# Expert gathers of the second table six steps behind the first table's, in place of four

## The chip, the cores and the metric

The kernel runs on one core of a Trainium2 chip. The metric is the device time of one execution in microseconds (us), lower is better. Engines are named as in the profile: PE is TensorE (matmul, with its weight loads as PEld), DVE is VectorE, ACT is ScalarE, POOL is GpSimd, SP is SyncE, which here only issues DMAs.

## What is computed

Two transformer layers over 256 tokens of width 2048. All but the last part is dense: convolution, attention, gating, feed-forward. The change touches only the last part, a layer of 16,384 one-neuron experts, cut here from the reference:

```python
top_s, top_pos = lax.top_k(cand, PEER_TOPK)              # 16 experts per head, 8 heads, each token
expert_idx = jnp.take_along_axis(cand_idx, top_pos, axis=-1)
gates = jax.nn.softmax(top_s, axis=-1).astype(xn.dtype)
...
u = jnp.take(expert_u, idx, axis=0)                      # one row of 2048 floats per expert
a = jnp.einsum('thkd,td->thk', u, xb)
hid = jax.nn.gelu(a) * g
vsel = jnp.take(expert_v, idx, axis=0)
return jnp.einsum('thk,thkd->td', hid, vsel)
```

So each token needs 128 rows of table u, a dot product with each, and then the same 128 rows of table v, weighted and summed.

## The kernel before

**Steps and groups.** 128 tokens lie on the partitions, and there are two such token tiles. One step k gathers one expert's row for each of 128 tokens: `gather_u(k)` brings 128 rows of table u into one of `NU` = 5 slots (`s_u`), `gather_v(k)` 128 rows of table v into one of `NV` = 7 slots (`s_v`). There are 256 steps; four steps are a group g, so group g has steps 4g to 4g+3, and there are 64 groups. Experts with a first key of 88 or more (5120 of them, 40 panels of 128) are not gathered: their rows are skipped by the bounds check, and they are computed densely for all tokens from panels that SP loads.

**What each engine does with a step.** DVE does `dot(k)`: two fused multiply-and-sum instructions over 1024 columns each (L1706), which also frees the u slot. After the four dots of a group, `dots_summed(g)` (L1718) lets ACT apply the gelu (L1097); DVE multiplies by the gates in `hidden(g)` (L1756), which stands behind the first dot of group g+1; ACT then spreads the result into small diagonal matrices, `spreads(g)` (L1050). PE does `adds(k)` (L2291), four matmuls with the v slot as the moving operand, which adds the weighted rows into PSUM and frees the v slot. The trace shows each such matmul as two rows, so one add is x8.

**What surrounds them on PE.** PE runs its program in order: iteration i is for the adds of group i-1. In iterations 0 to 16 the dense u panels stand between the adds (L2240, 40 of them), in iterations 18 to 31 the "token fours" (L2280, 64 of them, which make the gates of the dense experts), from iteration 34 on the dense v panels (L2250, 40 of them). I call these the first, the second and the third stage.

**The handshake of the second stage.** For each token four, DVE and ACT build one-hot operands. On DVE they stand between the dots, in program order. The part that the prediction turns on is `one_keys_late` (L1738), once in a group, behind dot 4g+1: it overwrites the buffer of the group before, and so waits on `one_key_used` until PE has run all token fours of iteration g-1. These stand behind the adds of group g-2, of which the last is add 4g-5. `gated` (L1749) has a similar wait.

```python
for q in range(4):                          # PE, iteration i
    if i >= 1:
        adds(4 * (i - 1) + q)
...
for f in token_fours_in(i)[-4:]:
    token_four(f)
```

**The order of the gathers.** POOL issues all gathers, in an order written out in one loop. `gather_u(k)` waits until dot k-5 has freed its slot (`dot_ready`), `gather_v(k)` until add k-7 has freed its slot (`v_used`). POOL stands still while it waits, and whatever stands behind waits too. `LAG` says how many steps `gather_v` runs behind `gather_u`:

```python
gather_u(0)
gather_v(0)
gather_v(1)
for k in range(1, ROUTES * TOPK + LAG):
    if k < ROUTES * TOPK:
        gather_u(k)
    for first in {4: (2, 3), 5: (4, 5), 6: (6,)}.get(k, ()):
        gather_v(first)
    if k >= LAG + NV:
        gather_v(k - LAG)
```

Of the kernel before, what the change touches and what calls it, by code (L numbers as in the profile page):

```python
# [214 lines left out]
def two_layers(nc, stream, dense_u, columns, x, meta, b_out, g_mix_post, g_ffn, g_ffn_post, g_norm1, g_norm2, w_forget,  # L215
# [9 lines left out]
    def place(name, shape, offset, dt=f32):  # L225
        assert name not in names
        names.add(name)
        return nc.alloc_sbuf_tensor_at(name, shape, dt, offset=offset)
# [95 lines left out]
    panel_early = [place(f"s_panel_early{i}", [128, D], S + k * K) for i, k in enumerate((60, 52, 32))]  # L324
    NE = len(panel_early)
    score = place("s_score", [128, TT * PH, 2 * NKEYS], S + 16 * K)
    NU, NV, NW, NH, BATCH, LAG = 5, 7, 4, 4, 4, 4
    ROUTES, GROUPS = TT * PH, TOPK // BATCH


# [2069 lines left out]
```

How the kernel before makes its waits and increments, by code:

```python
def wait(engine, semaphore, value):  # L209
    if not (isinstance(value, int) and value <= 0):
        engine.wait_ge(semaphore, value)
# [239 lines left out]
        @block.sync  # L452
# [2 lines left out]
            for t in range(TT):  # L455
                sp.dma_start(xres[:, t, :], x[t * 128:(t + 1) * 128, :]).then_inc(x_loaded[t], 16)
            sp.dma_start(cols[:, :], columns).then_inc(cols_loaded, 16)
            for s in range(4):
                sp.dma_start(raw[s][:, :], stream[s]).then_inc(raw_loaded[s], 16)
            panels = stream.rearrange("(q s) p n -> q s p n", s=4)
            with sp.Fori(1, NPANELS // 4) as q:
                for s in range(4):
                    sp.wait_ge(panel_used, q * 4 + (s - 4 + 1 + 1))
                    sp.dma_start(raw[s][:, :], panels[bass.ds(q, 1), s].rearrange("a p n -> (a p) n"))\
                        .then_inc(raw_loaded[s], 16)
            for d in range(NE, 2 * DENSE):
                if d == DENSE:
                    sp.wait_ge(panel_used, NPANELS + 1 + DENSE)
                    sp.dma_start(xn_late[:, :], put_by[0]).then_inc(xn_back, 16)
                    sp.dma_start(xres_late[:, :], put_by[1]).then_inc(xres_back, 16)
                if d < NE + 2:
                    sp.wait_ge(split_ready, NSPLITS - 3 + d - NE)
                else:
                    sp.wait_ge(panel_used, NPANELS + 1 + d + 1 - 2)
                src = dense_u[d] if d < DENSE else expert_v[(SPARSE + d - DENSE) * NKEYS:(SPARSE + d - DENSE + 1) * NKEYS, :]
```

## Time and profile before

| | us |
|---|---|
| median of 3 executions | 3002.77 (2999.91 to 3003.15) |
| the profiled execution, its own time | 3000.82 |
| its span in the trace | 2998.8 |
| PE busy in the span | 2758.8 (92%) |
| DVE busy | 1923.8 (64%) |
| ACT busy | 1178.2 (39%) |
| POOL busy | 652.6 (22%) |

Positions in the trace are microseconds from the start of the span. The first gather is issued at 1804.95 and the last at 2976.76, so the change can act only in the last 1,200 us. A row of a timeline reads: start, duration, engine, line, instruction, output<-input, count, and in square brackets how long the engine stood idle before it and what ended that. In a row of stages each engine has its busy time and number of instructions, then come the granted share of the TensorE clock, the mean busy share of the 16 DMA engines, and what they moved in GB/s.

### The profile page before, as it was taken

To read this page: it belongs to the slowest core of one execution; us is meant where nothing else is said; L and a number is where in the kernel's file an instruction comes from. 1 tells how busy PE (TensorE), PEld (TensorE's weight loads), DVE (VectorE), ACT (ScalarE), POOL (GpSimd) and SP (SyncE) were. 2 spreads that over 40 slices of the span, in tenths; PEclk is the share of its full clock that TensorE was granted. 3 is DMA by queue.
4 is the path that set the end of the run, shared out by engine and by line. 5 is a ranking of instruction groups with operands and counts; after the bars stand their busy time and mean duration, and the time that the engine had idled before them with its cause. 6 is when DMAs were issued, how large, how long until landed. Compare 5 with 4: busy or idle time off the path is not lost.

```text
span 2998.8 us, 45605 instructions
## 1 busy us (share of the span) xinstructions
PE 2758.8 (92%) x17100; PEld 2069.8 (69%) x17100; DVE 1923.8 (64%) x3184; ACT 1178.2 (39%) x2298; POOL 652.6 (22%) x568
## 2 busy tenths in 40 slices
PE   8999999999999997999999999999977887887884
PEld 7886788888888887989999889777754432222230
DVE  6888566556656565455444558987869875555555
ACT  1003443333334344435334444655556542222223
POOL 0000000000000000040000002444447664444453
PEclk9999999999999998999999999999977678998996
DMA  6333545555555553443455657999999999999998
GB/s 244 141 141 106 206 161 187 184 194 182 191 187 187 190 184 129 155 155 141 177 186 184 239 200 259 363 418 409 416 383 396 390 416 417 415 413 394 414 407 319
DMA packets 131299, 785.52 MB, mean 262 GB/s; under 512 B 34631, under 2 KB 34631, under 8 KB 35847
## 3 DMA queue, kind: packets, MB, share of 16 engines
q1 hardware_dynamic: 55424, 393.68, 35.6%
q0 software_dynamic: 75712, 389.74, 32.3%
q8 instruction: 94, 1.54, 0.2%
q14 instruction: 69, 0.56, 0.1%
HBM read 940.23 MB, written 4.19 MB: 315 GB/s over the span
## 4 chain that ended last, share of the span: by engine, by line
PE 57%; DMA 19%; DVE 12%; issue 7%; ACT 3%; POOL 2%; DVEq 1%; POOLq 0%; SPq 0%; ACTq 0%
DMA s_u<-in_expert_u,s_u_index 15%; PE bank L1847 10%; PE bank L1841 10%; PE bank L1842 10%; PE bank L1843 10%; PE bank L1848 5%; PE bank L1937 4%; PE bank L2240 4%; DVE s_u L1706 4%; DMA s_v<-in_expert_v,s_v_index 3%; PE bank L2291 2%; POOL s_u L585 2%; DVE s_cacc L1217 2%; DVE s_w_lo L1128 1%; DVE s_yrow L1390 1%
## 5 line engine op out<-in xcount | busy, mean ns | idle before, releaser
L1128 DVE TENSOR_TENSOR s_w_lo<-s_raw,s_w_hi 128x2048 fp32r<-128x2048 f32 x258 | 592.6, 2297 | 578.0 <-ACT s_w_hi L628 577.6
L628 ACT ACTIVATE s_w_hi<-s_raw 128x2048 fp32r<-128x2048 f32 x256 | 490.4, 1916 | 751.7 <-PE bank L1843 476.3
L1847 PE MATMUL bank<-s_a,s_w_hi 128*128 128x512 f32 x1408 | 493.8, 394 | 3.4 <-DVE s_w_lo L1128 3.2
L1706 DVE CUSTOM_DVE_ANT_0 s_u<-s_u,s_xn_late 128x1024 f32<-128x1024 f32 x256 | 303.7, 1224 | 244.0 <-DMA s_u<-in_expert_u,s_u_index 217.1
L2291 PE MATMUL bank<-s_v,s_spread 128*32 128x512 f32 x2048 | 310.3, 715 | 152.0 <-DMA s_v<-in_expert_v,s_v_index 121.6
L1050 ACT ACTIVATE s_spread<-s_ident,s_hid 32x32 f32<-32x32 f32 x1024 | 325.7, 318 | 205.0 <-DVE s_hid L1756 175.8
L1848 PE MATMUL bank<-s_a,s_w_lo 128*128 128x256 f32 x1408 | 394.8, 280 | 0.0
L585 POOL DMA_INDIRECT s_u<-in_expert_u,s_u_index x256 | 292.5, 1142 | 432.1 <-DVE s_halfdot L1706 267.9
L601 POOL DMA_INDIRECT s_v<-in_expert_v,s_v_index x256 | 309.9, 1211 | 191.7 <-PE bank L2291 109.6
L1706 DVE CUSTOM_DVE_ANT_0 s_u<-s_u,s_xn 128x1024 f32<-128x1024 f32 x256 | 303.8, 1224 | 56.0 <-DMA s_u<-in_expert_u,s_u_index 49.6
L1841 PE MATMUL bank<-s_a,s_w_hi 128*128 128x256 f32 x1152 | 325.3, 282 | 4.1 <-DVE s_a L1152 2.4
L1842 PE MATMUL bank<-s_a,s_w_hi 128*128 128x256 f32 x1152 | 324.6, 282 | 0.0
L1843 PE MATMUL bank<-s_a,s_w_lo 128*128 128x256 f32 x1152 | 324.2, 281 | 0.0
L1847 PEld LDWEIGHTS bank<-s_a,s_w_hi 128*128 128x128 f32 x1408 | 264.3, 188 | 66.5 <-DVE s_w_lo L1128 6.4
L2291 PEld LDWEIGHTS bank<-s_v,s_spread 128*32 128x32 f32 x2048 | 64.1, 119 | 345.0 <-issue 267.0
L2250 PE MATMUL bank<-s_raw,s_ha 128*32 128x512 f32 x2560 | 298.9, 616 | 0.2 <-DMA s_raw<-in_expert_v 0.2
L2240 PE MATMUL bank<-s_xnt,s_raw 128*128 128x256 f32 x1184 | 264.8, 382 | 2.9 <-ACT s_ha L1060 1.7
L1848 PEld LDWEIGHTS bank<-s_a,s_w_lo 128*128 128x128 f32 x1408 | 264.6, 188 | 0.4
L2240 PEld LDWEIGHTS bank<-s_xnt,s_raw 128*128 128x128 f32 x1184 | 222.1, 190 | 59.6 <-issue 28.2
L1937 PE MATMUL bank<-s_a_f,s_raw 128*128 128x272 f32 x1024 | 235.2, 393 | 2.1 <-DVE s_a_f L1185 1.4
L2250 PEld LDWEIGHTS bank<-s_raw,s_ha 128*32 128x32 f32 x2560 | 97.6, 115 | 201.6 <-issue 195.7
L1841 PEld LDWEIGHTS bank<-s_a,s_w_hi 128*128 128x128 f32 x1152 | 218.0, 189 | 8.5 <-issue 4.4
(321 smaller groups left out, 3821.8 us busy)
## 6 DMA issues: line engine op xcount, KB each, us to landing
s_raw<-in_stream SPq DMA_DIRECT2D x292, 1024.0 KB, 4.7
s_raw<-in_expert_v SPq DMA_DIRECT2D x40, 1024.0 KB
s_raw<-in_dense_u SPq DMA_DIRECT2D x37, 1024.0 KB
s_u<-in_expert_u,s_u_index POOLq DMA_INDIRECT x256
s_v<-in_expert_v,s_v_index POOLq DMA_INDIRECT x256
s_panel_early<-in_dense_u POOLq DMA_DIRECT2D x3, 1024.0 KB, 11.4
s_xres<-in_x SPq DMA_DIRECT2D x2, 1024.0 KB, 5.9
out<-s_out_row SPq DMA_DIRECT2D x32, 64.0 KB
```

The source lines that it names most:

```text
L628: act.activation(w_hi[s % 2][:, :], raw[s][:, :], ACT.Copy).then_inc(hi_ready, 1)
L1128: dve.tensor_tensor(w_lo[s % 2][:, :], raw[s][:, :], w_hi[s % 2][:, :].bitcast(f32), ALU.subtract)\
L1706: ins = dve.tensor_tensor_reduce(out=u_slot[k % NU][:, half], in0=u_slot[k % NU][:, half], in1=xn_late[:, half] if t else xn[:, 0, half], ...
L1841: pe.matmul(dst, left[0], right[0], start=start, stop=False)
L1842: pe.matmul(dst, left[0], right[1], start=False, stop=False)
L1843: return pe.matmul(dst, left[1], right[0], start=False, stop=stop)
L1847: pe.matmul(dst, left[0], both, start=start, stop=False)
L1848: return pe.matmul(dst[:, 0:T], left[1], both[:, 0], start=False, stop=stop)
L1937: ins = pe.matmul(bank[c][:, 0:L], raw[c % 4][:, k * 128:(k + 1) * 128], a_f[:, k, :], start=k == 0, stop=k == KT - 1)
L2240: ins = pe.matmul(bank[b][:, 0:T], source[:, k * 128:(k + 1) * 128], xnt[:, k, 0:T], start=k == 0, stop=k == KT - 1)
L2250: ins = pe.matmul(bank[4 * t + q][c * Q:(c + 1) * Q, :], ha[:, d, t * 128 + q * Q:t * 128 + (q + 1) * Q], raw[r][:, c * 512:(c + 1) * 512] ...
L2291: ins = pe.matmul(bank[4 * t + q][c * Q:(c + 1) * Q, :], spread[g % NW][:, q, :], v_slot[k % NV][:, c * 512:(c + 1) * 512], start=False, s ...
```

## The change

`LAG` goes from 4 to 6. Every `gather_v` from the eighth on (v7) is issued two steps of `gather_u` later, and the last six stand behind the last `gather_u`, where it was four. The first seven `gather_v`, the slots, the waits of each gather and all other engines' programs stay as they are.

```diff
     score = place("s_score", [128, TT * PH, 2 * NKEYS], S + 16 * K)
-    NU, NV, NW, NH, BATCH, LAG = 5, 7, 4, 4, 4, 4
+    NU, NV, NW, NH, BATCH, LAG = 5, 7, 4, 4, 4, 6
     ROUTES, GROUPS = TT * PH, TOPK // BATCH
```

What that makes of POOL's queue at the start, from `gather_u(9)` on, where `s_u0` to `s_u4` are the u slots (step k uses slot k modulo 5) and `s_v0` to `s_v6` the v slots (modulo 7). Before:

```order
L585 DMA s_u4_137<-in_expert_u,s_u_index2_177 128x2048
L585 DMA s_u0_133<-in_expert_u,s_u_index2_177 128x2048
L585 DMA s_u1_134<-in_expert_u,s_u_index2_177 128x2048
L601 DMA s_v0_138<-in_expert_v,s_v_index1_192 128x2048
L585 DMA s_u2_135<-in_expert_u,s_u_index0_175 128x2048
L601 DMA s_v1_139<-in_expert_v,s_v_index2_193 128x2048
L585 DMA s_u3_136<-in_expert_u,s_u_index0_175 128x2048
L601 DMA s_v2_140<-in_expert_v,s_v_index2_193 128x2048
```

The same place on POOL in the changed kernel:

```order
L585 DMA s_u4_137<-in_expert_u,s_u_index2_177 128x2048
L585 DMA s_u0_133<-in_expert_u,s_u_index2_177 128x2048
L585 DMA s_u1_134<-in_expert_u,s_u_index2_177 128x2048
L585 DMA s_u2_135<-in_expert_u,s_u_index0_175 128x2048
L585 DMA s_u3_136<-in_expert_u,s_u_index0_175 128x2048
L601 DMA s_v0_138<-in_expert_v,s_v_index1_192 128x2048
L585 DMA s_u4_137<-in_expert_u,s_u_index0_175 128x2048
L601 DMA s_v1_139<-in_expert_v,s_v_index2_193 128x2048
```

The gather v7 (slot `s_v0`) stood behind u11 (slot `s_u1`) and stands behind u13 (slot `s_u3`) now.

In the second stage, POOL's queue around v95 (slot `s_v4`), the last gather that the adds of group 23 need. Before:

```order
L585 DMA s_u4_137<-in_expert_u,s_u_index5_180 128x2048
L601 DMA s_v4_142<-in_expert_v,s_v_index4_195 128x2048
L585 DMA s_u0_133<-in_expert_u,s_u_index6_181 128x2048
L601 DMA s_v5_143<-in_expert_v,s_v_index5_196 128x2048
L585 DMA s_u1_134<-in_expert_u,s_u_index6_181 128x2048
L601 DMA s_v6_144<-in_expert_v,s_v_index5_196 128x2048
```

The same place in the changed kernel, which begins with the same `gather_u(99)`:

```order
L585 DMA s_u4_137<-in_expert_u,s_u_index5_180 128x2048
L601 DMA s_v2_140<-in_expert_v,s_v_index4_195 128x2048
L585 DMA s_u0_133<-in_expert_u,s_u_index6_181 128x2048
L601 DMA s_v3_141<-in_expert_v,s_v_index4_195 128x2048
L585 DMA s_u1_134<-in_expert_u,s_u_index6_181 128x2048
L601 DMA s_v4_142<-in_expert_v,s_v_index4_195 128x2048
```

v95 stood behind u99, which waits for dot 94; it stands behind u101 now, which waits for dot 96.

## Rows read from the trace of the kernel before

**Rows 1.** The page's first part: busy time of each engine.

```profile
PE 2758.8 (92%) x17100; PEld 2069.8 (69%) x17100; DVE 1923.8 (64%) x3184; ACT 1178.2 (39%) x2298; POOL 652.6 (22%) x568
```

**Rows 2.** Busy time by stage: start:end, length, engines, PE clock, DMA share, GB/s.

```profile
1880.00:1890.00 10.00, 8.30 (x46) 5.77 (x45) 9.05 (x25) 4.45 (x12) 3.01 (x4) 1.00 0.81 280
1890.00:1900.00 10.00, 10.00 (x54) 7.17 (x52) 9.21 (x30) 7.86 (x29) 3.84 (x5) 1.00 0.90 338
1900.00:2203.00 303.00, 301.52 (x1607) 218.13 (x1606) 242.80 (x663) 164.09 (x524) 145.46 (x125) 1.00 1.01 414
2240.00:2260.00 20.00, 18.79 (x124) 10.77 (x123) 15.96 (x30) 10.70 (x33) 9.63 (x8) 0.76 0.76 280
2260.00:2340.00 80.00, 62.85 (x370) 35.49 (x373) 77.06 (x147) 51.12 (x155) 62.52 (x46) 0.69 1.01 410
2425.00:2700.00 275.00, 227.87 (x1896) 71.95 (x1899) 154.57 (x288) 84.73 (x272) 145.14 (x128) 0.89 1.01 415
2700.00:2975.00 275.00, 210.32 (x1728) 64.99 (x1720) 152.64 (x282) 81.75 (x263) 135.73 (x122) 0.85 1.00 405
```

**Rows 3.** DMA queues and issues from 1900 to the end.

```profile
q0 software_dynamic: 70506, 358.67, 80.4%
...
s_v<-in_expert_v,s_v_index POOLq DMA_INDIRECT x246
s_u<-in_expert_u,s_u_index POOLq DMA_INDIRECT x242
...
s_xn_late<-put_by SPq DMA_DIRECT2D x1, 1024.0 KB, 8.4
```

**Rows 4.** Timeline of POOL at the start: v7 and v9.

```profile
1885.45 0.99 POOL L601 DMA_INDIRECT s_v<-in_expert_v,s_v_index  x1 [0.30 <-issue]
...
1896.19 0.99 POOL L601 DMA_INDIRECT s_v<-in_expert_v,s_v_index  x1 [0.30 <-issue]
```

**Rows 5.** Waits of POOL and PE, 1900 to 2203: total us, times, longest.

```profile
POOL s_v L601 <- PE bank L2291: 82.8, 25, 10.0
...
PE bank L2240 <- DMA s_raw<-in_dense_u: 1.2, 2, 0.7
```

**Rows 6.** Chain that ended last: two gathers of u, issue to landing.

```profile
2034.43 22.95 DMA s_u<-in_expert_u,s_u_index
...
2184.71 21.10 DMA s_u<-in_expert_u,s_u_index
```

**Rows 7.** Timeline of POOL, second stage: v91, v93, v95, v97.

```profile
2290.07 0.99 POOL L601 DMA_INDIRECT s_v<-in_expert_v,s_v_index  x1 [0.30 <-issue]
...
2295.31 1.97 POOL L601 DMA_INDIRECT s_v<-in_expert_v,s_v_index  x1 [0.31 <-issue]
...
2303.49 0.99 POOL L601 DMA_INDIRECT s_v<-in_expert_v,s_v_index  x1 [0.30 <-issue]
...
2309.33 1.97 POOL L601 DMA_INDIRECT s_v<-in_expert_v,s_v_index  x1 [0.30 <-issue]
```

**Rows 8.** Timeline of PE: adds 91 and 95 and the token fours behind them.

```profile
2302.31 1.07 PE L2291 MATMUL bank<-s_v,s_spread 128*32 128x512 f32 x8 [1.10 <-DMA s_v<-in_expert_v,s_v_index]
...
2305.11 1.96 PE L2280 MATMUL bank<-s_one_key,s_one_key_late 128*128 128x40 f32 x16
...
2316.23 1.94 PE L2291 MATMUL bank<-s_v,s_spread 128*32 128x512 f32 x8 [2.93 <-DMA s_v<-in_expert_v,s_v_index]
...
2321.53 3.61 PE L2280 MATMUL bank<-s_one_key,s_one_key_late 128*128 128x40 f32 x16
```

**Rows 9.** Timeline of DVE: `one_keys_late` of groups 24 and 25.

```profile
2310.37 1.21 DVE L1738 TENSOR_TENSOR s_one_key_late<-s_iota_f,s_slots_t 128x1024 f32<-128x1024 f32 x1
...
2325.41 1.22 DVE L1738 TENSOR_TENSOR s_one_key_late<-s_iota_f,s_slots_t 128x1024 f32<-128x1024 f32 x1
```

**Rows 10.** Chain that ended last: the last gather, v255, and its add.

```profile
2976.76 14.89 DMA s_v<-in_expert_v,s_v_index
...
2991.79 1.10 PE bank L2291 x8
```

## The prediction, on record before the changed kernel ran

> **What bounds the kernel now.** The first view is the page's busy time [rows 1]: PE is busy for 92% of the span and everything else far less, which says nothing about the last 1,200 us, where alone the change can act. So the second view is the busy time by stage [rows 2]. The reader is to see three different limits there. From 1900 to 2203, the stage with the dense u panels, PE is busy for 301.52 of 303 us, and the DMA engines are full at the same time (share 1.01, 414 GB/s). From 2260 to 2340, in the stage with the token fours, DVE is busy for 77.06 of 80 us, and the DMA engines are again full (410 GB/s). From 2425 on, PE and DVE have room, and the DMA engines alone are full (415 and 405 GB/s). Two stretches are not full: 1880 to 1900 (shares 0.81 and 0.90) and 2240 to 2260 (0.76).
>
> The third view is the list of DMA queues and issues [rows 3]: 358.67 MB in 246 + 242 gathers is 0.735 MB a gather, and at 414 GB/s that is 1.78 us of the DMA engines' time. A gather that isn't issued while they have room costs 1.78 us later, when they are full; the two steps of the change are worth 3.6 us. The fourth is the chain that ended last: a gather of u takes 22.95 and 21.10 us from its issue to its landing [rows 6], some twelve times its own transfer. The rest is queue. All gathers together move the same bytes before and after, so the end can only move by time in which the DMA engines have less to do than now, or more.
>
> **The change part by part.** No instruction is added or removed. Only `gather_v` moves, in POOL's queue, behind two more `gather_u`; SP's queue is not touched. I go through the stages.
>
> *Start.* v7 now issues at 1885.45. Its new place is behind u13, where v9 now issues at 1896.19 [rows 4], so v7 comes 10.7 us later, and each v after it similarly. The u gathers around it gain nothing, for there they wait for dots (DVE is busy 9.05 and 9.21 of 10 us). Two gathers less are moved while the DMA engines have room: a loss between 0 (they catch up before it matters) and 3.6 us. The queue fills at once afterwards, so I take more than half, +2 us.
>
> *First stage.* `gather_v` stands still for PE here 25 times, 82.8 us in total, up to 10.0 us [rows 5], and a `gather_u` behind it stands too. With the change two more `gather_u` are out before POOL stops. That looks like the gain, but PE has waited for its panels for only 1.2 us in this stage and the DMA engines are full, so neither has time to give back. What can change is the order: u rows come up to 3.6 us earlier against the same bytes, and the first dot of the second stage (u72, which takes 21.10 us to land) with them. Between 0 and -3.6 us; I take -1, since the start has taken away most of it. The adds keep up: a v gather is issued seven adds ahead, nearly two groups of PE's work, and two gathers less of lead leave them in time.
>
> *Second stage.* Here is the term that decides. Behind the first two dots of group g, `one_keys_late` waits until PE has run the token fours of iteration g-1, and these stand behind add 4g-5. Now gather v(4g-5) stands behind u(4g-1), which waits for dot 4g-6. With the change it stands behind u(4g+1), which waits for dot 4g-4. So a circle of seven dots becomes one of five: dot 4g-4, POOL's issue, the landing, the add, four token fours, `one_keys_late`. Is there room for that? For group 24, v91 issues at 2290.07, and its new place is where v93 stands, 2295.31: 5.2 us later [rows 7]. The add starts when v91 has landed, 2302.31, the fours end at 2305.11 + 1.96 = 2307.07 [rows 8], and DVE comes to `one_keys_late` at 2310.37 [rows 9]: 3.3 us of room, so 1.9 us late. For group 25, v95 goes from 2303.49 to v97's place at 2309.33, 5.8 us later; the add starts at 2316.23, the fours end at 2321.53 + 3.61 = 2325.14, DVE is there at 2325.41: 0.3 us of room, so 5.6 us late. The mean of these two is 3.8 us. What is queued behind `one_keys_late` on DVE is every later dot, so all `gather_u`, and behind those all `gather_v`.
>
> There are 11 such groups (21 to 31). The wait of group g depends on dot 4g-4, which is behind `one_keys_late` of group g-2 and ahead of that of group g-1, so delays add up over every second group: 5.5 x 3.8 = 21 us if the landing takes as long as now. That is the upper end. It will not: when DVE stalls, fewer gathers are under way, and they land sooner. Now v91 lands within 2302.31 - 2290.07 = 12.2 us and v95 within 12.7. The shortest 1 MB landing near this stage is 8.4 us, for `xn_late` [rows 3]. With 8.4, v91 is not late any more (1.9 - 3.8), v95 still 5.6 - 4.3 = 1.3 us: mean 0.6, 5.5 x 0.6 = 3.5 us. The lower end is 0, as nothing excludes that landings shorten by a little more. I take 6, nearer to the 8.4 us case. It can't be made good later, as the DMA engines are full to the end.
>
> Of a landing the Trainium skill gives another picture (DMA: Bandwidth & Descriptors, section on the anatomy of one DMA on the gpsimd path): a fixed 2.0 us and the bytes at 436 GB/s. By that page the estimate for a gather is 3.7 us, the stage would have room for two steps more, and this term would be 0. The rows don't agree with it for a full queue (12.2 to 22.95 us), though they may come nearer to it as the queue empties; this is what the second rival below rests on, by its own rows.
>
> *Third stage.* DMA-bound; PE waits little for spreads, and a v slot's round trip is seven steps in either kernel. 0. The bound for a gain: if the 405 GB/s of 2700 to 2975 rose to the 415 of the stretch before, 275 x (1 - 405/415) = 6.6 us.
>
> *End.* v255 is issued at 2976.76, lands 14.89 us later, and its add starts at 2991.79 [rows 10]. It waits for add 248. v248 comes two u gathers later in the queue, but u252, whose dot opens its group, two v gathers earlier. I take 0; at most +3.6.
>
> The sum is 2 - 1 + 6 + 0 + 0 = +7 us. Against the profiled execution's own time that is 3000.82 + 7 = 3007.8 us. The median of the runs shown is 2 us higher, 3002.77, so I predict 3002.77 + 7 = 3010 us. A difference of under 0.2% (6 us) is about what a measurement of this kernel can't tell from no change, and my forecast is just outside of it.
>
> **The rivals.**
> 1. *No change that can be told.* The landings of the second stage shorten by as much as the gathers come late, and the two gathers of the start are made good by the order. For it: v91 needs only 1.9 us. Against it: v95 needs 5.6, and DVE has only 3 us of room in 80. Time: 3002.8 to 3006, the start's 3.6 at most.
> 2. *Faster.* The two extra u gathers under way do what the first stage's waits suggest, and fill the hole of 2240 to 2260, where 20 x (1 - 0.76) = 4.8 us of DMA time are idle. With the 3.6 us of the first stage that is 3002.8 - 8.4 = 2994 us. For it: 82.8 us of POOL's waits. It decides if the idle DMA time before 2260 is smaller after than before and that of the second stage no larger. Against it: in that hole DVE waits in its handshake with PE, which two more gathers of u don't release.
> 3. *Much slower.* The landings stay at 12 us and the circle costs the full 21 us, with 2 more for the start: 3025 us. Against it: a DMA queue that is not fed can't stay as long as one that is.
>
> That the change does nothing at all is excluded by POOL's order, of which each place after v6 differs.
>
> **How the numbers follow.** I give my forecast (a moderate loss in the second stage) 0.38, rival 1 0.33, rival 2 0.17, rival 3 0.12. Slower by over 0.2%: rival 3 and nine tenths of the forecast, 0.46. Faster: 0.17. Within 0.2%: 0.37. The likeliest case by itself spans 3006 to 3015. The range goes from rival 2's price, 2994, to rival 3's, 3025, with about 1 in 10 beyond each.
>
> **What would show it.** In the changed kernel's profile: DVE's idle time ahead of `one_keys_late`, now next to nothing, is 5 us or more over the stage, released by PE's token fours; PE's idle time ahead of adds 91 and 95 ends with a landing; the landing of v95 takes 8 to 11 us in place of 12.7; the DMA share from 2260 to 2425 falls by 2 to 5%; the first stage's end on PE stays within 2 us; POOL's waits for PE in the first stage fall to under half. The prediction is wrong if DVE is not stalled there and the end moves all the same, or if PE, in the first stage, comes to wait for v gathers, which I have put at nothing.

## The result, and the profile after

The changed kernel takes 3024.61 us (median of 6 runs, 3022.07 to 3026.43) against 3001.84 us before (6 runs on the same chip, 2999.67 to 3003.15). The ratio is 1.0076, with a 95% interval of 1.0066 to 1.0087: slower by 22.8 us, or 20 to 26. I had forecast slower, by 7 us. The direction and the place are right, and the size is a third of what came. The time lies 0.4 us inside the upper end of my range, 3025, and that end was the price of a rival whose mechanism did not come. That the range holds is luck.

The profiled execution took 3025.01 us, with a span of 3023.0 us. The page's busy time, which answers to [rows 1], does not show the loss: every engine does the same work.

```profile
PE 2780.3 (92%) x17100; PEld 2075.3 (69%) x17100; DVE 1922.3 (64%) x3184; ACT 1178.6 (39%) x2298; POOL 654.0 (22%) x568
```

The busy time by stage does. These rows of the changed kernel answer to [rows 2], with the same columns (start:end, length, five engines, PE clock, DMA share, GB/s).

```profile
1880.00:1890.00 10.00, 8.38 (x47) 5.84 (x46) 9.12 (x25) 4.40 (x11) 2.02 (x3) 1.00 0.75 259
1890.00:1900.00 10.00, 10.00 (x55) 7.33 (x54) 9.13 (x30) 7.93 (x29) 2.87 (x4) 1.00 0.82 282
1900.00:2203.00 303.00, 298.57 (x1579) 217.04 (x1581) 242.67 (x663) 163.94 (x524) 141.43 (x125) 1.00 1.01 411
2203.00:2260.00 57.00, 43.43 (x228) 27.50 (x228) 37.46 (x71) 28.15 (x83) 20.31 (x19) 0.61 0.84 326
2260.00:2340.00 80.00, 62.02 (x336) 33.24 (x330) 70.95 (x133) 48.94 (x149) 54.93 (x42) 0.64 0.97 373
2340.00:2425.00 85.00, 63.89 (x332) 33.28 (x328) 70.41 (x136) 47.48 (x142) 55.39 (x44) 0.60 0.94 365
```

And two windows of the kernel before that the prediction had not read:

```profile
2203.00:2260.00 57.00, 37.10 (x233) 24.93 (x229) 43.19 (x80) 32.74 (x98) 25.19 (x22) 0.67 0.90 353
2340.00:2425.00 85.00, 65.76 (x350) 34.29 (x342) 75.03 (x142) 49.35 (x148) 58.05 (x48) 0.62 0.99 394
```

The reader is to see three things. In the start, from 1880 to 1900, the DMA engines move 259 and 282 GB/s in place of 280 and 338, which is 0.77 MB or about one gather less, and in the first stage 411 in place of 414. From 2203 to 2425 they move much less: 326, 373 and 365 GB/s in place of 353, 410 and 394. And DVE, busy for 77.06 of 80 us before, is busy for 70.95: it waits. From 2260 to 2425 the same 165 us carried this many bytes, before (first row) and after (second row), from the view of DMA:

```profile
DMA packets 13024, 66.28 MB, mean 402 GB/s; under 512 B 4941, under 2 KB 4941, under 8 KB 4941
```

```profile
DMA packets 12012, 60.81 MB, mean 369 GB/s; under 512 B 4597, under 2 KB 4597, under 8 KB 4597
```

The difference of 5.47 MB is 13.6 us of work at 402 GB/s, and nothing can give it back, since the DMA engines are full (share 1.00 to 1.01) from 2425 to 2975 in both kernels. The share of busy time fell by only 4 to 5 points, worth 7.5 us: it understates a loss that the bytes show.

What the engines waited for is in the view of waits from 2200 to 2480 (total us, times, longest). First DVE and PE of the kernel before:

```profile
DVE s_ha L1749 <- PE bank L2280: 9.1, 7, 2.6
DVE s_one_key_late L1738 <- PE bank L2280: 2.3, 2, 2.0
...
PE bank L2291 <- DMA s_v<-in_expert_v,s_v_index: 26.0, 15, 2.9
```

And of the changed one:

```profile
DVE s_ha L1749 <- PE bank L2280: 35.6, 10, 8.7
DVE s_one_key_late L1738 <- PE bank L2280: 3.0, 2, 2.0
...
PE bank L2291 <- DMA s_v<-in_expert_v,s_v_index: 60.1, 32, 6.9
```

So DVE waits 26.5 us longer for PE's token fours, and PE 34.1 us longer for the v rows of the adds that stand ahead of them. The stall is not at `one_keys_late`, where the prediction had looked for it, but at `gated` (L1749), which waits for the first two of the same four fours and is reached earlier, behind the first dot of the group. POOL's waits for PE ahead of `gather_v`, which had looked like the case for the change, are gone, but POOL now waits for dots instead. These rows are of the changed kernel from 1900 to 2203 and answer to [rows 5]:

```profile
POOL s_u L585 <- DVE s_halfdot L1706: 113.0, 47, 4.2
...
POOL s_u L585 <- PE bank L2291: 22.6, 9, 4.0
...
PE bank L2291 <- DMA s_v<-in_expert_v,s_v_index: 3.6, 4, 1.3
POOL s_v L601 <- PE bank L2291: 3.2, 2, 2.1
```

Before, the same view had 43.6 and 10.2 us in the places of 113.0 and 22.6. 82.8 us of waiting at `gather_v` have become 3.2, but the three waits together are 137 us before and 139 after. POOL's waiting has moved from `gather_v` to `gather_u`, and the kernel is slower.

### The profile page after: what moved, and what is told of

Its sections match the earlier page's. It is cut to its first block, busy times and chain, and to the rows that moved or that the text cites. A ratio compares the mean times of both kernels' runs of the same rounds, so it can differ in the third digit from the quotient of the medians.

```text
span 3023.0 us, 45605 instructions
## 1 busy us (share of the span) xinstructions
PE 2780.3 (92%) x17100; PEld 2075.3 (69%) x17100; DVE 1922.3 (64%) x3184; ACT 1178.6 (39%) x2298; POOL 654.0 (22%) x568
## 4 chain that ended last, share of the span: by engine, by line
PE 53%; DMA 21%; DVE 14%; issue 7%; POOL 2%; ACT 2%; DVEq 1%; POOLq 0%; SPq 0%; another core or an unknown queue 0%; ACTq 0%
DMA s_u<-in_expert_u,s_u_index 13%; PE bank L1847 10%; PE bank L1841 10%; PE bank L1842 10%; PE bank L1843 10%; DMA s_v<-in_expert_v,s_v_index 8%; PE bank L1848 5%; DVE s_u L1706 5%; PE bank L1937 4%; POOL s_u L585 2%; DVE s_cacc L1217 2%; PE bank L2291 2%; PE bank L2280 1%; DVE s_w_lo L1128 1%; PE bank L2250 1%
## 5 line engine op out<-in xcount | busy, mean ns | idle before, releaser
L2291 PE MATMUL bank<-s_v,s_spread 128*32 128x512 f32 x2048 | 321.2, 733 | 178.6 <-DMA s_v<-in_expert_v,s_v_index 170.4
L1847 PEld LDWEIGHTS bank<-s_a,s_w_hi 128*128 128x128 f32 x1408 | 264.8, 188 | 66.2 <-DVE s_w_lo L1128 6.4
L1937 PEld LDWEIGHTS bank<-s_a_f,s_raw 128*128 128x128 f32 x1024 | 194.4, 190 | 43.3 <-issue 3.4
```

The lines of the kernel that those rows point to most:

```text
L1847: pe.matmul(dst, left[0], both, start=start, stop=False)
L1937: ins = pe.matmul(bank[c][:, 0:L], raw[c % 4][:, k * 128:(k + 1) * 128], a_f[:, k, :], start=k == 0, stop=k == KT - 1)
L2291: ins = pe.matmul(bank[4 * t + q][c * Q:(c + 1) * Q, :], spread[g % NW][:, q, :], v_slot[k % NV][:, c * 512:(c + 1) * 512], start=False, s ...
```

## The experiments

In all of them the edit is in the order of POOL's gathers, of PE's token fours, or both. Times are medians, with the range and the number of runs behind, and a time that another is set against is that of the kernel before, on the same chip. The ratio with its 95% interval is an estimate of its own and not the quotient of the two medians; by it the differences from the kernel before are up to 2 us larger. Where dots are timed, the time is the end of the dot in the one trace of the kernel.

**Which stage costs it.** Three kernels have lag 6 in one stage only and lag 4 elsewhere. The loop becomes, for the second stage:

```diff
-    if k >= LAG + NV:
-        gather_v(k - LAG)
+    while next_v < ROUTES * TOPK and k >= next_v + (6 if 72 <= next_v < 128 else 4):
+        gather_v(next_v)
+        next_v += 1
```

The condition of the other two is `next_v < 72` (start and first stage) and `next_v >= 128` (third stage). The two added lines move later line numbers by 2, so that L1749 is L1751 there.

> Six steps behind for v72 to v127 alone (the gathers that the adds in the second stage need), four for all others. Circle theory (DVE's handshake with the token fours waits for adds whose gathers come two steps later): this part alone costs 15 us (dots 80 to 128 took 188.1 us after the change, 172.9 before), so 3001.8 + 15 = 3017 us, with DVE's idle time ahead of L1749 and L1738 near 35 us. Rival (the start's late gathers leave a debt that the full DMA engines never pay back): within 4 us of before.

> Six steps behind for v7 to v71 alone, four from v72 on. Circle theory: dot 80 came 5.2 us later after the change, because groups 18 and 19 have the handshake too; with v72 and later issued in the old order part of that comes back, so 3 to 5 us slower, 3005 to 3007. Rival (debt of the start): all of the loss is here, 3020 or more. Third possibility (more gathers of the first table under way in the first stage help): under 3000.

> Six steps behind for v128 to v255 alone. Circle theory: no handshake here, the stage is bound by the DMA engines, so nothing up to its end; at the end v255 waits for add 248, whose gather now stands behind u254, and the trace after shows 4.4 us there: 3003 to 3007 us. Rival (two steps later cost the same everywhere, in proportion to the steps): half of 22.8 us, 3013.

Measured: second stage alone 3021.1 us (3020.06 to 3023.08, 5) against 3003.31, ratio 1.0065 [1.0051, 1.0079], +18 us; start and first stage alone 3006.21 (3004.87 to 3008.29, 11), ratio 1.0012 [1.0003, 1.0021], +3 us; third stage alone 3004.63 (3002.33 to 3006.37, 11), ratio 1.0005 [0.9996, 1.0014], +1.3 us and not told apart from nothing. The sum of the three, 22, is the whole loss of 22.8, so within their intervals they don't help or hide one another. Four fifths of it is the 56 gathers of the second stage. Its waits, from 2200 to 2480, are those of the changed kernel:

```profile
DVE s_ha L1751 <- PE bank L2282: 32.4, 11, 5.9
```

**Half of the change.** `LAG` is 5, halfway between the kernel before and the changed one.

```diff
-    NU, NV, NW, NH, BATCH, LAG = 5, 7, 4, 4, 4, 4
+    NU, NV, NW, NH, BATCH, LAG = 5, 7, 4, 4, 4, 5
```

> Five steps behind everywhere. Circle theory: the circle gets one dot shorter, not two; room was 3.3 us for group 24 and 0.3 us for group 25 against a step of 3.6 us, so groups are late by 0.3 and 3.3 us in place of 1.9 and 5.6, about half: 3001.8 + 8 to 12 = 3010 to 3014 us. Rival (a threshold between five and six): within 4 us of before.

Measured: 3007.0 us (3006.16 to 3010.17, 11) against 3003.31, ratio 1.0018 [1.0009, 1.0027], +4 us. This is less than the 8 to 12 us that I had expected, and inside what the rival, a threshold between five and six, gave. The first step costs 4 us, the second 19: the loss has a knee, as a circle with some slack in it must. DVE's wait at `gated` is between the two, and has grown by 13 us where the kernel lost 4, so this wait does not by itself measure the loss:

```profile
DVE s_ha L1749 <- PE bank L2280: 22.5, 10, 4.7
```

**Giving the circle its two steps back on PE.** If the loss comes from the token fours standing behind adds whose gathers have become later, it must go away when the fours are moved ahead of those adds, with the gathers left at lag 6. In one pair of kernels the fours of iteration 20 and later stand ahead of all four adds, in the other between the second and the third add. Each has a control with `LAG = 4`. The edit of the second pair, on PE:

```diff
     for q in range(4):
         if i >= 1:
             adds(4 * (i - 1) + q)
         if q == 1:
+            for f in token_fours_in(i) if i >= 20 else range(0):
+                token_four(f)
...
-    for f in token_fours_in(i)[-4:]:
+    for f in token_fours_in(i)[-4:] if i < 20 else range(0):
         token_four(f)
```

> Six steps behind, and in PE's iterations 20 to 31 the four token fours stand ahead of the four adds, so those that the handshake of group g waits for stand behind add 4g-9 in place of 4g-5. Circle theory: four steps of room are given back where two were taken, and the cost of the second stage (18 us in the run of that stage alone) goes away: within 5 us of the same order with four steps behind, and 3003 to 3010 us if that order costs nothing of its own. Rival (the second stage loses because gathers of the second table reach the DMA queue late, whatever PE does with them): still 15 to 20 us over the same order with four steps behind.

> The control of the last: the same order of PE, four steps behind. Circle theory: the order itself may cost, since add 4g-4 now waits for fours that need dot 4g+3, while v(4g+3) stands in POOL's queue behind the wait for add 4g-4: 3002 to 3015 us. What counts is the distance between the two, 5 us or less by the circle theory, 15 to 20 by its rival.

> Six steps behind, and in PE's iterations 20 to 31 the four token fours stand between the second and the third add, so those that the handshake of group g waits for stand behind add 4g-7 in place of 4g-5: exactly the two steps given back that the change took. Circle theory: the second stage is as long as before (dots 80 to 128 in 170 to 176 us), what is left is the cost outside of it, 4 to 5 us by the runs of the other stages alone: 3005 to 3009 us. Rival (fours ahead of all adds only hid the loss, for it had a different loop of its own): 3012 us or more.

> The same place of the fours with four steps behind. Circle theory: the handshake has two steps of room more than before, but adds 4g-2 and 4g-1 now stand behind fours that need dot 4g+3, and gathers v(4g+5) and v(4g+6), which need the slots of these adds, stand in POOL's queue ahead of u(4g+10) and u(4g+11). Two of the four adds are caught in this in place of four, so the cost should be well under that of fours ahead of all adds (15 us): 3000 to 3008 us. If the first circle alone counted it would be faster than before, by up to 4 us.

Measured, with the fours ahead of all adds: lag 6 takes 3008.52 us (3006.53 to 3011.2, 9) against 3002.39, ratio 1.0024 [1.0014, 1.0034]; lag 4 takes 3017.25 (3015.49 to 3019.84, 5), ratio 1.0053 [1.0039, 1.0067], 2 us above the bound that I had given. With the fours between the adds: lag 6 takes 3008.0 (3006.92 to 3009.81, 11) against 3002.05, ratio 1.0021 [1.0012, 1.003]; lag 4 takes 3000.82 (2998.44 to 3005.77, 11), ratio 0.9998 [0.9989, 1.0007], no difference.

So lag 6 costs 22.8 us with the fours behind the adds, 7 us with them in the middle, and with them ahead of all adds it is 9 us faster than lag 4. The sign of the same edit depends on where the fours stand. I had expected the two kernels with the fours ahead within 5 us of each other, and had not foreseen that lag 6 would be the faster one. In the traces the time from dot 80 to dot 128 shows the loss come and go: 173.0 us before, 188.1 changed, 171.9 with lag 6 and the fours ahead, 171.8 with lag 6 and the fours between. With lag 4 and the fours ahead it is 184.0. The second stage of lag 6 with the fours between, the window 2260 to 2340, is full again, as [rows 2] had it (1.01, 410):

```profile
2260.00:2340.00 80.00, 65.31 (x372) 37.99 (x368) 76.88 (x148) 51.72 (x156) 62.20 (x47) 0.66 1.01 410
```

Of the 6 us that this kernel still takes more than the one before, the other stages had 4 when measured by themselves. What the control with lag 4 lost when the fours stood ahead of all adds looks like a second loop of the same kind, read from its waits and not tested by itself. The adds now stand behind fours whose one-hot operands come late, hold their v slots longer, and `gather_v` waits. In the view of waits of POOL, from 2200 to 2480, lag 4 and then lag 6 (the kernel before has 11.2 us in the first row's place):

```profile
POOL s_v L601 <- PE bank L2291: 38.2, 13, 7.1
```

```profile
POOL s_u L585 <- PE bank L2291: 13.5, 11, 2.4
POOL s_v L601 <- PE bank L2291: 2.1, 3, 1.4
```

**The other direction.** `LAG = 3` everywhere, and lag 3 for the second stage only (the loop above with `3 if 72 <= next_v < 128 else 4`).

> Three steps behind everywhere. Circle theory: the handshake gets one dot more of room, but the idle time ahead of L1749 is only 9.1 us before, and the DMA engines are full, so little is left to win: 2 to 5 us faster at best, 2997 to 3003 us. Rival (the wait for the v slots, 82.8 us in the first stage, grows and holds back the first table's gathers, so four is a best value between two slopes): 5 to 15 us slower.

> Three steps behind for v72 to v127 alone, four for the others. Circle theory: 0 to 4 us faster, 2998 to 3002 us, with the idle time ahead of L1749 under the 9.1 us of before. Rival (gathers stopped by the v slots): slower by 3 us or more, and in this run all in the second stage.

Measured: 3006.78 us (3004.84 to 3011.05, 10) against 3002.39, ratio 1.0019 [1.0009, 1.0028], +4.4 us; and 3003.18 (3002.26 to 3006.53, 11), ratio 1.0005 [0.9996, 1.0014], no difference. In the second kernel DVE's wait at `gated` falls from 9.1 us to almost nothing:

```profile
DVE s_ha L1751 <- PE bank L2282: 2.9, 2, 2.8
```

It buys nothing: those 6 us of DVE time lay beside full DMA engines. I had expected up to 5 us faster with lag 3 everywhere and up to 4 with lag 3 in the second stage, and both failed: lag 4 is between two slopes. Where lag 3 loses is open. With lag 3 in the second stage alone the interval runs to 4 us, and in the traces dots 80 to 128 take 175.6 us there and 176.2 with lag 3 everywhere, against 173.0, so part of it may be in the second stage after all. From 1860 to 3010 its waits of `gather_v` for PE are longer (here lag 3, then before), but which of them costs the 4.4 us I have not shown.

```profile
POOL s_v L601 <- PE bank L2291: 139.9, 41, 10.0
```

```profile
POOL s_v L601 <- PE bank L2291: 109.6, 36, 10.0
```

**The start by itself.** Lag 6 for v7 to v39, 4 behind (`6 if next_v < 40 else 4`).

> Six steps behind for v7 to v39 alone, four from v40 on, while PE is still in the first stage. This measures the start's term by itself (two gathers fewer under way while the DMA engines have room), which the prediction put at 2 us, between 0 and 3.6. Theory: the debt is paid back before the first stage ends, as PE sets the pace there, so 0 to 1 us, 3002 to 3003 us. Rival (the 3 us of the run with the first stage alone are this debt): 3005 us or more.

Measured: 3004.01 us (3002.27 to 3008.15, 11) against 3002.05, ratio 1.0008 [0.9999, 1.0017], +2 us, between 0 and 5. It agrees with the +2 of the prediction, but doesn't exclude 0 or 3.6, and lies between the 0 to 1 us that I expected here and the rival's 3. In its trace dot 72 ends 3.4 us later than before and dot 128 3.9 later. The other kernels with lag 4 up to there spread over 2.6 us at dot 72, so this too is a hint, that the debt is not paid back in the first stage, and no proof.

## Why the direction was right and the size was not

**The second stage: the circle is real, its size was too small.** The term was +6 us, from a range of 0 to 21; it measured 18 us (the kernel with lag 6 there alone). That the circle of dot, gather, add, fours and DVE's wait carries the loss rests on three results: it is there with lag 6 in this stage alone, it goes away when the fours stand two adds earlier, and it is little with one step. The kernel's own rows show where one turn of the circle goes. The first rows are from DVE's timeline of the changed kernel: `gated` of group 24 and of group 26.

```profile
2319.95 0.49 DVE L1749 TENSOR_TENSOR s_ha<-s_ha,bank 128x320 f32<-128x320 f32 x1 [4.74 <-PE bank L2280]
...
2351.47 0.49 DVE L1749 TENSOR_TENSOR s_ha<-s_ha,bank 128x320 f32<-128x320 f32 x1 [4.87 <-PE bank L2280]
```

The next are from the chain that ended last: v99, its add and the first two fours, x16, that the second of them waits for (a matmul shows as two rows, so a four is x8).

```profile
2335.79 10.00 DMA s_v<-in_expert_v,s_v_index
2345.79 0.14 issue
2345.93 1.94 PE bank L2291 x8
2347.86 3.58 PE bank L2280 x16
2351.47 0.49 DVE s_ha L1749
```

On POOL these two rows belong to it, the issue of u102 and, seven gathers later, that of v99:

```profile
2324.51 1.15 POOL L585 DMA_INDIRECT s_u<-in_expert_u,s_u_index  x1 [5.76 <-DVE s_halfdot L1706]
...
2335.79 1.97 POOL L601 DMA_INDIRECT s_v<-in_expert_v,s_v_index  x1 [0.30 <-issue]
```

From the release of DVE at 2319.95 to the issue of v99 are 15.84 us: 4.56 until dot 97 is done and POOL issues u102, and 11.28 in which POOL issues one gather after another, each of 0.99 to 1.98 us and 0.30 behind the last. Dot 100, which u105 waits for, ends at 2333.18, when POOL is only coming to v98 (2333.20), so it is as much POOL's issuing as DVE's work that sets this part. The landing takes 10.00 us, 0.14 go by until PE starts, and add 99 and the two fours take 5.5. Together they are 31.5 us for two groups, which is the distance of the two rows. Before, two groups took less. These are the first and the last `one_keys_late` of groups 21 to 31, before and then after:

```profile
2269.58 1.21 DVE L1738 TENSOR_TENSOR s_one_key_late<-s_iota_f,s_slots_t 128x1024 f32<-128x1024 f32 x1
...
2414.03 1.22 DVE L1738 TENSOR_TENSOR s_one_key_late<-s_iota_f,s_slots_t 128x1024 f32<-128x1024 f32 x1
```

```profile
2276.46 1.22 DVE L1738 TENSOR_TENSOR s_one_key_late<-s_iota_f,s_slots_t 128x1024 f32<-128x1024 f32 x1
...
2435.73 1.22 DVE L1738 TENSOR_TENSOR s_one_key_late<-s_iota_f,s_slots_t 128x1024 f32<-128x1024 f32 x1
```

Ten groups took 144.45 us before, 28.9 for two, and 159.27 after, 31.9 for two. That is 3.0 us for each pair, 14.8 in all. My forecast had the right number of pairs and, in effect, 1.1 us for each.

Two steps of the sum failed, the landing and the mean. The mechanism held (landings shorten when DVE stalls), but I took 8.4 us for the shorter landing, from a 1 MB transfer of another queue, where the circle settles at 10.00. In the prediction's own example v91 now lands 9.86 us after its issue in place of 12.2:

```profile
2304.42 9.86 DMA s_v<-in_expert_v,s_v_index
```

With 12.2 - 9.86 = 2.4 us gained against 1.9 needed by v91 and 5.6 by v95, the two groups are 0 and 3.2 us late, and not 0 and 1.3. The second step is that I took the mean of the two groups and charged it for every second group. A delay of one group is also room for the next, which comes later itself, so a pair costs what the later of the two costs. The changed kernel shows it: `gated` waits 4.74 us in group 24, 4.87 in 26 and 4.91 in 28, and not at all in 25 and 27 (behind 28 the order changes, and 29 and 31 wait). The mean of 0 and 3.2, times 5.5 pairs, is only 9 us, so the landing alone does not explain what came. The larger, 3.2 for a pair, stands beside the measured 3.0, and gives 18 us, where 14.8 came. By the same rule 8.4 us of landing would have given 1.3 for a pair, or 7 us, and the landing as it was 5.6, or 31: the 21 us that I had called the upper end was none. That the larger counts is read from these waits, and no run tests it by itself.

Why the landing is 10 and not 8.4 can be read from the gathers beside it, though no run sets it apart. After each stall POOL issues its gathers in one burst. An add for which PE waited starts 8.94 us after the issue of v97, 8.68 after that of v98 and 10.14 after that of v99, and 8.34, 9.02 and 9.99 after those of v89, v90 and v91. So about 8.4 us does occur, but for the gathers ahead in the burst, and the fours wait for the last one of the group. I had put in the best case where the worst was needed.

PE's clock is a part of the circle. An add and two of the token fours (x16) come in a long and a short form in both kernels (1.94 with 3.61 us, and 1.07 with 1.96 [rows 8]). From 2316 to 2323 of the changed kernel, with the long form, the granted clock is 0.50, and from 2329.8 to 2331.5, with the short one, 1.00, the lower and the higher of the clock's two levels, 1.2 and 2.4 GHz. Over the stage the difference to the kernel before is little: the granted clock from 2260 to 2340 fell from 0.69 to 0.64, and one row of the two kinds of fours took 340 and 356 ns on the mean from 2260 to 2425 before, and 363 and 361 after, which for 32 of them is 0.5 us a group. But the mean hides that the fours ahead of each of DVE's six waits from 2285 on are in the long form, as here ahead of the wait in group 24, while those ahead of group 25, where DVE does not wait, are in the short one:

```profile
2314.41 1.94 PE L2291 MATMUL bank<-s_v,s_spread 128*32 128x512 f32 x8 [1.63 <-DMA s_v<-in_expert_v,s_v_index]
2316.28 3.64 PE L2280 MATMUL bank<-s_one_key,s_one_key 128*128 128x40 f32 x16
...
2329.74 1.98 PE L2280 MATMUL bank<-s_one_key,s_one_key 128*128 128x40 f32 x16
```

With the short form the turn of 31.5 us would be 2.5 us shorter, 29.0, nearly the stage's own pace of 28.9. That is an estimate from these rows. My 5.6 us for v95 was read with the long form, but no run holds the clock, so how much of the loss goes by it is open.

**The first stage: put at -1, it costs.** The chain of reasons was partly right. The first dots of the second stage do come earlier: by the ends of the instructions in the trace, dot 72 ends at 2205.1 in place of 2208.2 us. But by dot 80 the changed kernel is 5.2 us behind (2257.3 against 2252.1), and the kernel with lag 6 only up to v71 is 5.8 behind. What lies between is the same circle in its first turn, with a landing that has not shortened at all: v71 is issued at 2207.31, just behind the first stage, and by the chain of work that ends in this wait it takes 24.98 us. On the timeline of PE of the changed kernel, three adds wait for gathers of v, and the fours stand behind them:

```profile
2224.71 1.93 PE L2291 MATMUL bank<-s_v,s_spread 128*32 128x512 f32 x8 [0.93 <-DMA s_v<-in_expert_v,s_v_index]
...
2228.75 1.94 PE L2291 MATMUL bank<-s_v,s_spread 128*32 128x512 f32 x8 [2.10 <-DMA s_v<-in_expert_v,s_v_index]
...
2232.42 1.93 PE L2291 MATMUL bank<-s_v,s_spread 128*32 128x512 f32 x8 [1.74 <-DMA s_v<-in_expert_v,s_v_index]
2234.29 3.64 PE L2280 MATMUL bank<-s_one_key,s_one_key 128*128 128x40 f32 x16
```

The same fours of the kernel before started 6.5 us earlier, with no such waits ahead of them:

```profile
2227.78 1.98 PE L2280 MATMUL bank<-s_one_key,s_one_key 128*128 128x40 f32 x16
```

And on DVE of the changed kernel `gated` waits for these fours:

```profile
2237.96 0.49 DVE L1749 TENSOR_TENSOR s_ha<-s_ha,bank 128x320 f32<-128x320 f32 x1 [8.68 <-PE bank L2280]
```

Before, the longest such wait of the stage was 2.6 us. I had counted eleven groups for the circle, 21 to 31, and left out 18 to 20, because the window 2240 to 2260 already had holes. And PE did come to wait for v gathers in the first stage, 3.6 us, which I had put at nothing and had named as a sign that the prediction is wrong: PE is the limit there together with DMA, and add 63 ends at 2194.8 in place of 2191.3. "Two gathers less of lead leave them in time" failed four times. Start and first stage together measured +3 us (interval 1 to 6) where I had +1; of this the start alone may be the 2 that I gave it.

**Third stage and end.** I had 0 and 0, at most +3.6; lag 6 there alone measured +1.3 us, not told apart from nothing. The traces don't settle it. From dot 128 to the end are 573.7 us before and 577.6 in the changed kernel, and 576.6 to 577.2 in the three others with lag 6 there, but two kernels with lag 4 there have 576.9 and 579.4. The way from dot 255 to the end is 3.1 us longer (14.7 before, 17.8 after; the 4.4 us in an expectation above do not come out of the ends of the dots). It would be longer without any loss, since two more gathers of v, worth 3.6 us, stand behind the last dot. The chain that ended last shows this way: v255's gather waits for add 248, whose own gather takes 19.56 us.

```profile
2981.10 19.56 DMA s_v<-in_expert_v,s_v_index
...
3000.80 1.97 PE bank L2291 x8
...
3003.60 13.56 DMA s_v<-in_expert_v,s_v_index
...
3017.30 1.10 PE bank L2291 x8
```

So a loss near my bound of 3.6 us is neither confirmed nor excluded, by the traces or by the median of the kernel that has this edit alone (interval -1 to 4).

**The rivals.** "No change" (3002.8 to 3006) fell with a loss of 20 us or more. "Faster" fell with the hole of 2240 to 2260: the DMA engines moved 280 GB/s there before and 214 after.

```profile
2240.00:2260.00 20.00, 18.34 (x107) 13.27 (x110) 17.56 (x33) 4.74 (x15) 8.49 (x8) 0.62 0.64 214
```

"Much slower" had the right time, 3025 us, but by a landing that stays at 12 us and by the mean of the two groups, two errors of opposite sign. The landing went to 10, the groups that I had counted lost 14.8 us, and the rest came from the groups ahead of them and from the other stages. The Trainium skill's picture of a landing (DMA: Bandwidth & Descriptors, the anatomy of one DMA on the gpsimd path) gives the estimate of 3.7 us for a gather, from which no loss would follow (rival 1, though the prediction says the second). It is again not met: even in the less full queue the chain has 9.86 and 10.00 us.

**What was to show it.** DVE's idle time of 5 us or more ahead of `one_keys_late`, released by the fours: no, 3.0 against 2.3; it came ahead of `gated`, 26.5 us more. PE's idle time ahead of adds 91 and 95 ends with a landing: yes. The landing of v95 at 8 to 11 us: it is issued at 2317.76 and its add starts at 2328.74, so at most 10.98. The DMA share down by 2 to 5%: yes, and the bytes by 8%. The first stage's end on PE within 2 us: no, 3.5. POOL's waits for PE under half: yes, 25.8 of 93.0 with those ahead of `gather_u`.

## What to carry to other kernels

A wait that is gone is worth nothing unless its engine, or what it feeds, had time to give back: here 80 us of POOL's waits only moved from `gather_v` to `gather_u`, and while they stood at `gather_v` the v gathers were issued early. Before two gather streams are moved against each other, look for the circle that runs through every engine (here dot, issue, landing, add, fours, dot), write down its length beside the stage's own pace per turn, and solve for the landing time at which both fit, in place of taking the best landing that the trace shows. Where two turns of a circle interlock, the later one sets the pace, and their mean does not. Look at each wait on the same semaphore, since the stall shows at the first one in program order, and compare bytes moved, not the busy share, where DMA is the limit.

## What was not expected of the hardware

The time of a gather from issue to landing depends steeply on how full the queue is, and little of it is its own transfer. It is 21 to 23 us in the first stage, at 414 GB/s. At 410 GB/s, from 2260 to 2340 of the kernel before, it is 10.5 to 12.7 us for the gathers that PE waited for (v87, v91, v95), and at 373 GB/s, in the same window of the changed kernel, 8.3 to 11.0 (v89 to v91, v95 and v97). So 9% fewer bytes per microsecond went with about 2 us less for each landing. A busy share of 0.94 to 0.97 of the DMA engines went with 365 to 373 GB/s, where 0.99 went with 394: the share alone doesn't tell how many bytes are being lost.
